# Modulation products in pairs: two units in every second slot of the first attention, the second adding to the first's PSUM bank

## What is computed

```
proj = jnp.einsum('bsd,de->bse', h, w_in[l])          # first block: q, k, v, gates
...
mod = silu_c @ ada_w[layer] + ada_b[layer]            # second block, layer 0 and 1
shift_m, scale_m, gate_m, shift_f, scale_f, gate_f = jnp.split(mod, 6, axis=-1)
```

## Time and profile before

| | |
|---|---|
| median of 3 runs | 1061.81 us (1061.55 to 1061.92) |
| the profiled execution | 1061.61 us |
| its span in the trace | 1059.9 us |
| granted TensorE clock, mean | 0.998 |
| TensorE busy | 1042.0 us, 98% |
| VectorE busy | 774.3 us, 73% |
| ScalarE busy | 582.5 us, 55% |
| GpSimd busy | 66.6 us, 6% |
| read from HBM | 217.80 MB, 207 GB/s over the span |

### The profile page before, as it was taken

One profiled execution on the slowest core, in us unless ns is written; L12 is line 12 of the kernel. 1 busy time (PEld: TensorE's weight loads), 2 busy tenths in 40 slices (PEclk: granted clock), 3 DMA queues, 4 the chain that ended last, 5 costly groups with the idle time before them and its releaser, 6 DMA issues.

```text
span 1059.9 us, 21420 instructions
## 1 busy us (share of the span) xinstructions
PE 1042.0 (98%) x9022; PEld 996.2 (94%) x9022; DVE 774.3 (73%) x1138; ACT 582.5 (55%) x889; POOL 66.6 (6%) x78
## 2 busy tenths in 40 slices
PE   8999999999999999999999999999999999999997
PEld 8988889999999999997788999999899999999996
DVE  6467777765576768987867999977688768677642
ACT  6555666565445675545757555533545456565432
POOL 2000000000010514000110000000000010000000
PEclk9999999999999999999999999999999999999999
DMA  9656757655755684444667888867768676555621
GB/s 285 201 183 235 239 161 234 182 188 182 242 167 163 192 226 149 134 156 161 207 226 243 282 288 271 291 245 289 257 218 284 201 237 201 190 168 192 226 80 40
DMA packets 166955, 220.29 MB, mean 208 GB/s; under 512 B 4513, under 2 KB 147261, under 8 KB 166860
## 3 DMA queue, kind: packets, MB, share of 16 engines
q1 hardware_dynamic: 165338, 215.41, 62.2%
q0 software_dynamic: 832, 1.65, 0.8%
q10 hardware_dynamic: 690, 1.86, 0.5%
HBM read 217.80 MB, written 1.11 MB: 207 GB/s over the span
## 4 chain that ended last, share of the span: by engine, by line
PE 83%; DVE 12%; ACT 2%; issue 2%; DMA 0%; DVEq 0%; ACTq 0%
PE psG L585 20%; PE psG L587 19%; PE psG L586 19%; PE psS L585 4%; DVE wlo L1887 4%; PE psS L587 4%; PE psS L586 4%; PE psG L740 1%; DVE arow L1964 1%; PE psG L713 1%; PE psG L715 1%; PE psG L726 1%; PE psS L875 1%; PE psX L891 1%; DVE fz L2464 1%
## 5 line engine op out<-in xcount | busy, mean ns | idle before, releaser
L1887 DVE TENSOR_TENSOR wlo<-raw,whi 128x1024 fp32r<-128x1024 f32 x309 | 373.7, 1247 | 99.8 <-ACT whi L1271 94.5
L585 PE MATMUL psG<-Hlo,whi 128*128 128x256 f32 x1420 | 404.5, 285 | 1.9 <-DVE Hlo L1928 0.9
L587 PE MATMUL psG<-Hhi,whi 128*128 128x256 f32 x1420 | 400.2, 282 | 0.0
L586 PE MATMUL psG<-Hhi,wlo 128*128 128x256 f32 x1420 | 400.0, 282 | 0.0
L1271 ACT CAST whi<-raw 128x1024 fp32r<-128x1024 f32 x309 | 312.2, 1048 | 115.3 <-PE psG L587 30.0
L585 PEld LDWEIGHTS psG<-Hlo,whi 128*128 128x128 f32 x1420 | 268.4, 189 | 5.6 <-issue 3.1
L586 PEld LDWEIGHTS psG<-Hhi,wlo 128*128 128x128 f32 x1420 | 268.4, 189 | 0.0
L587 PEld LDWEIGHTS psG<-Hhi,whi 128*128 128x128 f32 x1420 | 268.4, 189 | 0.0
L585 PE MATMUL psS<-Glo,whi 128*128 128x256 f32 x316 | 89.8, 284 | 0.0
L587 PE MATMUL psS<-Ghi,whi 128*128 128x256 f32 x316 | 89.1, 282 | 0.0
L586 PE MATMUL psS<-Ghi,wlo 128*128 128x256 f32 x316 | 89.1, 282 | 0.0
(11 more groups left out here) (454 smaller groups left out, 1776.7 us busy)
## 6 DMA issues: line engine op xcount, KB each, us to landing
raw<-in_ada_w_dram SPq DMA_DIRECT2D x48, 1024.0 KB, 5.6
raw<-in_ffn_w_up_dram SPq DMA_DIRECT2D x44, 1024.0 KB, 5.2
raw<-in_w_in_dram SPq DMA_DIRECT2D x28, 1024.0 KB, 6.7
raw<-in_ev_w_in_dram SPq DMA_DIRECT2D x26, 1024.0 KB, 5.4
raw<-in_ffn_w_down_dram SPq DMA_DIRECT2D x22, 1024.0 KB, 5.0
raw<-in_od_w_in_dram SPq DMA_DIRECT2D x12, 1024.0 KB, 7.8
raw<-in_w_in_dram SPq DMA_DIRECT2D x11, 512.0 KB, 6.7
raw<-in_w_o_dram SPq DMA_DIRECT2D x4, 1024.0 KB, 5.1
```

The source lines that it names most:

```text
L585: mm(o, a_hi, b_lo, start=first, stop=False, skip_group_check=shared)
L586: mm(o, a_lo, b_hi, start=False, stop=False, skip_group_check=shared)
L587: return mm(o, a_hi, b_hi, start=False, stop=last, skip_group_check=shared)
L1887: V.tensor_tensor(ring_half(wlo, v, h - H0[v]), src, ring_half(whi, v, h - H0[v]).bitcast(F32), ALU.subtract).then_inc(lo_split, 1)
```

## The change

The units A0 to A7 no longer stand one to a slot. Slots 1, 3, 5 and 7 end with two of them (the second's place is called "slot1+" and so on), slots 0, 2, 4 and 6 with none. The second of a pair opens no bank: its products go on adding in the bank of the first (`start` only for the first unit, `stop` only for the second), and there is one copy for the pair, into quarter q // 2 of the row. So a part has two partial rows rather than four, and GpSimd's first addition of the fold falls away for parts 0 and 1. The list from unit 6 on now reads: va1 qb1 A0 A1 kvb qc0 A2 A3 qc1 kc0 fc A4 A5 kc1 vc0 A6 A7 vc1 G0 ga0 G1 ga1 G2 and on as before. Unit 25 is ga0 still, unit 21 is A6.

```diff
+PAIRED = (0, 1)
+ADA_PLACES = {0: ("slot1", "slot1+", "slot3", "slot3+"), 1: ("slot5", "slot5+", "slot7", "slot7+"),
...
         ada(f"slot{s}")
+        ada(f"slot{s}+")
...
+    SECOND = [SPAN[f"ada_{ADA_PLACES[n][q]}"][0] for n in PAIRED for q in (1, 3)]
+    banked = [int(k[0] not in "DG" and u not in IN_NORM + SECOND) for u, k in enumerate(UNITS)]
...
         def ada_out(u):
+            if u in SECOND:
+                return bank(u - 1)
...
-                    if u not in IN_NORM:
+                    if u not in IN_NORM + SECOND:
                         open_bank(u)
...
-                                      w[:, k, j * 256:(j + 1) * 256], start=(k == 0), stop=(k == 1))
+                                      w[:, k, j * 256:(j + 1) * 256], start=(k == 0 and u not in SECOND),
+                                      stop=(k == 1 and u + 1 not in SECOND))
...
                     n, q = ada_part(u)
+                    if u + 1 in SECOND:
+                        continue
...
+                    if u in SECOND:
+                        nc.scalar.copy(ada_row(n)[:, q // 2 * 256:(q // 2 + 1) * 256], ada_out(u)[:, 0:256]
+                                       ).then_inc(bank_free[B0[u - 1] % 2], 1)
+                        act.wait_ge(bank_free[B0[u - 1] % 2], B0[u - 1] // 2 + 1)
...
-                step(G.tensor_tensor(r[:, 0:512], r[:, 0:512], r[:, 512:1024], ALU.add))
+                if n not in PAIRED:
+                    step(G.tensor_tensor(r[:, 0:512], r[:, 0:512], r[:, 512:1024], ALU.add))
```

More of the change, by code:

```diff
@@ L64 @@
 ADA_ORDER = (0, 1, 2, 3, 4, 5, 6, 7, 8, 10, 9, 11)
-ADA_PLACES = {0: ("slot0", "slot1", "slot2", "slot3"), 1: ("slot4", "slot5", "slot6", "slot7"),
+PAIRED = (0, 1)
+ADA_PLACES = {0: ("slot1", "slot1+", "slot3", "slot3+"), 1: ("slot5", "slot5+", "slot7", "slot7+"),
               2: ("slot8", "slot9", "slot10", "slot11"), 3: ("hg7a", "hg7b", "na0a", "na1a"),
@@ L174, in build @@
     IN_NORM = [u for i in range(3) for q in "ab" for u in SPAN[f"ada_tail{i}{q}"]]
-    banked = [int(k[0] not in "DG" and u not in IN_NORM) for u, k in enumerate(UNITS)]
+    SECOND = [SPAN[f"ada_{ADA_PLACES[n][q]}"][0] for n in PAIRED for q in (1, 3)]
+    banked = [int(k[0] not in "DG" and u not in IN_NORM + SECOND) for u, k in enumerate(UNITS)]
     B0 = [sum(banked[:u]) for u in range(NU)]
@@ L1290, in keep_rows @@
                     n, q = ada_part(u)
+                    if u + 1 in SECOND:
+                        continue
                     act.wait_ge(ada_done, ON_PE.index(u) + 1)
                     row = ada_row(n)[:, q * 256:(q + 1) * 256]
-                    if u in IN_NORM:
+                    if u in SECOND:
+                        nc.scalar.copy(ada_row(n)[:, q // 2 * 256:(q // 2 + 1) * 256], ada_out(u)[:, 0:256]
+                                       ).then_inc(bank_free[B0[u - 1] % 2], 1)
+                        act.wait_ge(bank_free[B0[u - 1] % 2], B0[u - 1] // 2 + 1)
+                    elif u in IN_NORM:
                         nc.scalar.copy(row, ada_out(u)[:, 0:256]).then_inc(norm_row, 1)
@@ L1498, in _ @@
                     keep_rows(f"slot{s}")
+                    keep_rows(f"slot{s}+")
             ahead(SPAN["gm_a0"][0])
```

## The result

| | before | after |
|---|---|---|
| median of 20 runs each | 1061.55 us (1061.28 to 1062.32) | 1063.38 us (1063.02 to 1063.83) |
| ratio, 95% interval | | 1.0017 (1.0011 to 1.0023) |
| span of the profiled execution | 1059.9 us | 1061.4 us |
| granted TensorE clock, mean | 0.998 | 0.998 |

A forecast was written before the change was run, and what follows sets the result against it. TensorE, busy 98% of the span, was taken to bound the kernel. Pairs -0.56, the old wait -0.16 and new waits of +1.4 and +1.5 gave +2.2 us, so 1064.0 us; range 1062.0 to 1066.2 us.

The forecast's parts named there:

- vc1 lands: Load that ScalarE needs first in slot 7: third behind A6 and A7, landing at 115.1, bounds 114.5 and 116.7.
- second transposes of slot 7, wait: TensorE in slot 7: transposes start at 119.0 after a wait of 1.4 us, where 0.16 stood.
- ga0 issued, time to landing: Load for slot 8: issued at 124.3 after A6's products, not at 115.30, landing 5.4 us later at 129.7.
- second transposes of slot 8, wait: TensorE in slot 8: transposes start at about 132.6 rather than 130.35, after a wait of 1.5 us.
- -0.56: Modulation products on TensorE: each of four pairs saves 0.14 us, 0.56 us in all, on the path.
- 0.16: TensorE's old wait before the second transposes of slot 7, taken off the sum as 0.16 us.
- The fit of the Trainium skill: DMA rule for loads: 3 MB take 9.2 us, so vc1 lands at 113.0, in time, and only ga0 is late.
- Only ga0 late: Rival: vc1 lands by 113.6, slot 7 has no wait, slot 8's transposes start at 131.2; +0.8 us, 1062.6; chance 0.12.
- No load late: Rival: no load stops slots 7 and 8, and the pairs pay; -0.7 us, 1061.1; chance 0.12.
- slower loads: Rival: late loads take G0's 7.1 us; one gives +4.0 us, 1065.8, both +5.8, 1067.6; chance 0.12.
- The shared bank: A pair's second unit adding onto the first's bank on TensorE: priced at nothing, no bank opened later than now.
- Copies and folds: Four copies of 0.37 us leave ScalarE, two additions of 1.29 us leave GpSimd: worth nothing on the path.

The follow-up runs named there:

- swap_g0: The changed kernel with only ga0's load moved ahead of G0's: 1061.85 us, against 1061.47 for the kernel before.
- swap_a7: The changed kernel with only vc1's load moved ahead of A7's: 1062.21 us, against 1061.47 for the kernel before.
- swap_both: The changed kernel with vc1 loaded ahead of A7 and ga0 ahead of G0: 1060.52 us, against 1061.47 for the kernel before.
- own_banks: The changed kernel with the pairs in the same slots, but each unit opening its own bank: 1064.00 us, against 1061.45 for the kernel before.
- hold_ga0: The kernel before, with only ga0's load held until A7 is done: 1065.57 us, against 1061.47 without the hold.
- hold_qc1: The kernel before, with only qc1's load held until kvb's projection is done: 1061.44 us, against 1061.45 without the hold.
- even_sum6: The changed kernel with pairs in slots 0, 2, 4, 6 and part 0's sum in slot 6: median 1062.74 us, against 1061.47 for the kernel before.
- hold_less: The kernel before, with ga0's load held until the group product of slot 7: 1063.05 us, against 1061.47 without the hold.

## Why the prediction was right

**The place and the mechanism** held in every step of both loads. Both waits stand where they were forecast, ScalarE waits for the DMA ahead of its casts in just those slots, and swap_g0, swap_a7 and swap_both take away each and both.

| step | forecast | measured |
|---|---|---|
| pair of slot 5 starts, A6 issued | 102.68, 103.81 | 102.65, 103.78 |
| vc1 lands | 115.1 | 114.8 |
| second transposes of slot 7, wait | 119.0, 1.4 | 118.70, 1.21 |
| ga0 issued, time to landing | 124.3, 5.4 | 123.93, 5.3 |
| second transposes of slot 8, wait | 132.55, 1.5 | 132.26, 1.38 |
| ga1 lands | 135.7 | 135.5 |
| total | +2.2 | +1.83 |

The forecast's own sum with the measured waits, -0.56 - 0.16 + 1.21 + 1.38 = +1.87, gives the measured total.

**The sizes.** The median came out 0.6 us under the forecast 1064.0. Of this, 0.26 is the base: the kernel before, run again beside the changed one, took 1061.55 and not 1061.81. Another 0.3 is vc1's landing, which sets the start of both second transposes: A6, A7 and vc1 landed at 109.28, 111.9 and 114.8. The first took 5.5 us, not 5.3, and a further MB 2.7 and 2.8 us, where I took 3.0 from the row of A7 and vc1. That it came so near is in part luck. The same third load took 3.6 us more than the second in own_banks, and ga1 behind G1 took 3.6 in the changed kernel itself; the rows had shown a spread of 2.7 to 3.8, which I had no reason for and which no run here explains.

**The class.** I put 0.50 on slower by over 0.2% and 0.44 on no difference of that size. It is +0.17%, on the lower side of the line that the forecast's centre lay on; on which side it would fall was open.

**The fit of the Trainium skill.** "DMA: Bandwidth & Descriptors" (Anatomy of one DMA), with 2.0 us plus bytes over 436 GB/s, gave 113.0 for vc1's landing as an estimate, and by it slot 7 would have had no wait. The trace does not agree: vc1 landed at 114.8, and the wait was 1.21 us. The measurement decides.

**The rivals.** Only ga0 late (forecast +0.8) is what swap_a7 makes of the kernel, at +0.7. No load late (-0.7) is swap_both, at -0.95. What my list of rivals lacked is the clock: I priced slower loads at their own length, +4.0 and +5.8 us. In hold_ga0 one wait of 2.28 us came with a loss of 4.1, so the range of this rival was probably drawn too low; no run made such a load late in the changed kernel.

**A term at nothing.** The shared bank, priced at nothing, is worth about 0.5 us in slot 5, found only by taking it away. The sum is not off by it: it took 0.86 us for the second unit of every pair, and in slot 5 that holds only because the second needs no bank of its own. The reason was missing, not the number.

**Copies and folds** were rightly worth nothing: 1.8 us less on ScalarE and 2.7 us less on GpSimd left no trace in any wait.

## What to carry to other kernels

Where loads pass through a ring in order, a change in the order of work is a change of what each load waits for: write out both lists, and compare for every unit the one whose slot it takes, past the units that move. A load's lateness costs only through what stands behind it on the waiting engine, so follow that to the engine that bounds the kernel, as hold_qc1 (a cast 3.57 us late, nothing lost) and hold_ga0 (3.72 us late, 4.1 us lost) show side by side. If an edit pays in one place and loses by the order of loads, as here, move the load in the list and keep the edit: that gave the fastest kernel of this study, 1060.52 us.

## What the runs showed of the hardware

- TensorE's granted clock fell from 1.00 to 0.50 about 0.9 us after the end of a wait of 2.28 us (hold_ga0) and of one of 2.01 us (even_sum6), at a cost of some 1.7 and 1.6 us. After single waits of 1.19 to 1.62 us (hold_less, the changed kernel, swap_g0, swap_a7, own_banks) it stayed at 1.00 in the stretches behind them. In hold_ga0 all five executions lay within 0.3 us of each other; those of even_sum6 split into two groups 1.3 us apart.
- Two modulation units (16 column-tiled instructions each) cost 1.86 us together and one alone 1.00, so the second adds 0.86.
- A 1 MB load sent when nothing else of the ring was under way landed after 5.3 us (ga0) or 5.5 us (A6). One directly behind another landed 2.7 to 2.8 us after it (A7, vc1), but 3.6 us after it for ga1 behind G1 and for vc1 in own_banks. G0's load took 7.1 us with nothing ahead of it in the kernel before. Why these differ is open.
